# A SwiGLU feed-forward in two phases on Trainium2: gate and up of all columns first, then the down products as seven block products with seven open sums in PSUM

## What is computed

```python
def swiglu(h, w_in, w_out):
    gate, up = jnp.split(h @ w_in, 2, axis=-1)
    return (jax.nn.silu(gate) * up) @ w_out

cond = jax.nn.silu(c)
for l in range(DEPTH):
    mod = cond @ ada_w[l] + ada_b[l]
    sh0, sc0, gt0, sh1, sc1, gt1, sh2, sc2, gt2 = jnp.split(mod, 9, axis=-1)
    h = modulate(rms_norm(x, norm_g[l, 0]), sh0, sc0)
    x = x + (0.5 * (1 + gt0))[:, None, :] * swiglu(h, ffn_w_in[l, 0], ffn_w_out[l, 0])
    ...
    h = modulate(rms_norm(x, norm_g[l, 2]), sh2, sc2)
    x = x + (0.5 * (1 + gt2))[:, None, :] * swiglu(h, ffn_w_in[l, 1], ffn_w_out[l, 1])
```

## Time and profile before

| | us |
|---|---|
| three runs of the kernel before | 1482.46, 1481.02, 1480.61 |
| median | 1481.02 |
| span of the profiled execution (its time apart from the span is not listed; the three runs lie 0.6 to 2.5 above the span) | 1480.0 |
| TensorE matmul busy | 1457.4 (98%) |
| weight loads busy | 1327.5 (90%) |
| VectorE busy | 996.7 (67%) |
| ScalarE busy | 269.8 (18%) |
| SP's queue moved | 211.12 MB in 287168 packets |

### The profile page before, as it was taken

One profiled execution on the slowest core, in us unless ns is written; L12 is line 12 of the kernel. 1 busy time (PEld: TensorE's weight loads), 2 busy tenths in 40 slices (PEclk: granted clock), 3 DMA queues, 4 the chain that ended last, 5 costly groups with the idle time before them and its releaser, 6 DMA issues.

```text
span 1480.0 us, 27488 instructions
## 1 busy us (share of the span) xinstructions
PE 1457.4 (98%) x11800; PEld 1327.5 (90%) x11800; DVE 996.7 (67%) x1973; ACT 269.8 (18%) x542; POOL 74.7 (5%) x141
## 2 busy tenths in 40 slices
PE   6999999999999999999999999999999999999998
PEld 3999999888988989999989999988898889899997
DVE  6489987788534657888866767777963445555455
ACT  2100002442223030000030000035222311100001
POOL 7001110000000000000100000000000000000000
PEclk9999999999999999999999999999999999999999
DMA  9899998343422567898856878644342248356550
GB/s 335 259 292 298 306 304 230 111 128 100 115 59 87 177 194 236 274 301 270 282 180 213 276 242 273 200 132 142 114 115 59 60 143 274 117 184 192 174 170 30
DMA packets 306233, 282.93 MB, mean 191 GB/s; under 512 B 15368, under 2 KB 269696, under 8 KB 306112
## 3 DMA queue, kind: packets, MB, share of 16 engines
q1 hardware_dynamic: 287168, 211.12, 47.6%
q0 software_dynamic: 17952, 69.21, 13.7%
q10 hardware_dynamic: 992, 0.85, 0.2%
HBM read 280.10 MB, written 1.05 MB: 190 GB/s over the span
## 4 chain that ended last, share of the span: by engine, by line
PE 96%; DMA 1%; DVE 1%; ACT 1%; SPq 1%; issue 0%; ACTq 0%; DVEq 0%
PE ps L1600 95%; DMA arena<-in_ada_w_dram 1%; PE ps L1604 1%; SPq L485 1%; DVE arena L1458 0%; ACT rs L618 0%; ACT hT L618 0%; DVE x L1002 0%; DVE hT L970 0%; DVE hT L1585 0%; DVE arena L1453 0%; ACT xn L618 0%; ACTq L237 0%; SPq L483 0%; SPq L482 0%
## 5 line engine op out<-in xcount | busy, mean ns | idle before, releaser
L1600 PE MATMUL ps<-hT,ring 128*128 128x128 f32 (+2 forms) x2528 | 427.5, 322 | 3.8 <-ACT hT L618 3.8
L1600 PEld LDWEIGHTS ps<-hT,ring 128*128 128x128 f32 (+1 forms) x2528 | 371.7, 191 | 49.5 <-issue 10.7
L1600 PE MATMUL ps<-arena,ring 128*128 128x256 f32 (+2 forms) x1712 | 372.7, 370 | 0.0
L1600 PEld LDWEIGHTS ps<-arena,ring 128*128 128x128 f32 x1712 | 309.2, 190 | 36.7
L1600 PE MATMUL ps<-y_both,arena 128*128 128x128 f32 x1920 | 228.5, 275 | 0.0
L1600 PEld LDWEIGHTS ps<-y_both,arena 128*128 128x128 f32 x1920 | 221.1, 192 | 0.2
L939 DVE SCALAR_TENSOR_TENSOR ada_acc<-ada_stage,cond,ada_acc 128x512 f32<-128x512 f32 x231 | 173.6, 751 | 9.0 <-DMA ada_stage<-in_ada_w_dram 1.1
L1028 DVE TENSOR_TENSOR arena<-arena,ps 128x256 f32<-128x256 f32 x80 | 33.5, 419 | 171.6 <-ACT arena L661 171.6
L1600 PE MATMUL ps<-y_both,ring 128*128 128x128 f32 (+1 forms) x896 | 140.5, 305 | 0.0
L1600 PEld LDWEIGHTS ps<-y_both,ring 128*128 128x128 f32 x896 | 126.2, 191 | 6.4
L661 ACT ACTIVATE arena<-ps 128x128 f32<-128x128 f32 x80 | 22.2, 278 | 577.7 <-PE ps L1600 577.7
(11 more groups left out here) (280 smaller groups left out, 1172.4 us busy)
## 6 DMA issues: line engine op xcount, KB each, us to landing
ring<-in_ffn_w_in_dram SPq DMA_DIRECT2D x176, 512.0 KB, 5.4
ada_stage<-in_ada_w_dram POOLq DMA_DIRECT2D x66, 1024.0 KB, 6.9
ring<-in_ffn_w_out_dram SPq DMA_DIRECT2D x88, 512.0 KB, 6.7
ring<-in_mix_w_in_dram SPq DMA_DIRECT2D x46, 512.0 KB, 5.1
ring<-in_mix_w_in_dram SPq DMA_DIRECT2D x12, 1024.0 KB, 5.3
ring<-in_mix_w_in_dram SPq DMA_DIRECT2D x6, 1536.0 KB, 6.4
ring<-in_mix_w_out_dram SPq DMA_DIRECT2D x8, 1024.0 KB, 5.2
arena<-in_ada_w_dram SPq DMA_DIRECT2D x6, 1024.0 KB, 17.2
```

The lines of the kernel that those rows point to most:

```text
L1600: return nc.tensor.matmul(out_, lhsT, rhs, start=start, stop=stop, **kw)
```

## The change

Each half is cut in two phases, and chunks go by **pairs** (256 hidden columns).

- Phase 1 makes gate and up of all 22 chunks. The first two are done plainly, the other ten pairs by seven block products of eight matmuls each (the same matmuls as before, two chunks at a time, in four PSUM banks; two sets of four banks take turns). The weight sums are 128 x 1024 now and made in two parts (`weight_sums(..., late)`), and the results stay in SBUF, in the new `hidT` of 22 tiles.
- Phase 2 makes the down products by the same block scheme: a pair of chunks is the inner dimension, two halves of the 1024 outputs and two halves of the tokens are the others. So a pair takes 7 x 4 = 28 matmuls of 128 tokens, where it took 16 of 256. Each of the seven products accumulates over the eleven pairs in its own PSUM bank and is combined only once, at the end (`residual`). VectorE makes four sums of weight blocks a pair (`down_sums`, 128 x 512) and the token sums of `hidT` (`t_sums_of`, in four batches).
- The last three pairs' products are reordered so that the seven sums close one after another.
- `ring` becomes 12 cells of 1024 elements: an up pair takes four, a down pair two, the mixer's blocks three. There are eight landing semaphores instead of four.
- The units of `ada_w` become 256 x 1024 elements (still 1 MB), two sweeps of 128 x 1024 each; they stand at eleven steps of phase 1 and seven of phase 2 (`ADA_PLACES`).
- Small tiles move to other memory (`parts`, `sil`, `scaled`, `final_diag`).

```diff
-SLOTS = 4
+PAIRS_FF = NC // 2
+STEPS = PAIRS_FF + 1
+RING_CELLS = 12
...
+T_BATCHES = ((0, 3), (3, 7), (7, 10), (10, 11))
...
+ADA_PLACES = [("up", s, 4.4) for s in range(1, STEPS)] + [("down", p, 2.4) for p in range(7)]
...
             def ffn(l, half):
-                for c in range(NC):
-                    chunk(l, half, c)
+                for p in range(PAIRS_FF):
+                    use, col = up_use(half, p), 2 * P * p
+                    room(l, use)
+                    win = ffn_w_in[l:l + 1, half, :, :].rearrange("a (k p) (g n) -> p (a k) g n", p=P, g=2)
+                    for g in range(2):
+                        sp.dma_start(up_weights(l, half, p)[:, :, g, :], win[:, :, g, col:col + 2 * P])\
+                          .then_inc(full_of(l, use), 16)
+                for p in range(PAIRS_FF):
+                    use, row = down_use(half, p), 2 * P * p
+                    room(l, use)
+                    sp.dma_start(view(slot(l, use, 2048), 2, D),
+                                 ffn_w_out[l:l + 1, half, row:row + 2 * P, :].rearrange("a (c p) n -> p (a c) n", p=P))\
+                      .then_inc(full_of(l, use), 16)
...
+            def ffn_up(l, half, before):
+                for s in range(STEPS):
...
+                        link(l, V.tensor_tensor(parts[:, 0:2, :], parts[:, 7:8, :].broadcast_to([P, 2, 2 * P]),
                                                 both[:, 1:5:3, :], ALU.add))
...
+                        free(V.tensor_tensor(parts[:, 5, :], parts[:, 2, :], both[:, 5, :], ALU.add),
+                             f"combined {half}" if p == PAIRS_FF - 1 else None)
+                        weight_sums(l, half, p + 2, 0)
...
+                    weight_sums(l, half, p + 2, 1)
+                    if p == PAIRS_FF - 2:
+                        for q in range(2):
+                            down_sums(l, half, q)
+                    if p == 7:
+                        t_sums_of(l, half, 0)
+                    ada_at(l, half, "up", s)
+
+            def ffn_down(l, half):
+                t_sums_of(l, half, 1)
+                for p in range(PAIRS_FF - 2):
+                    dv.wait_ge(*PE.at(l, f"sums read {half} {p}"))
+                    down_sums(l, half, p + 2)
+                    if p == 3:
+                        t_sums_of(l, half, 2)
+                        t_sums_of(l, half, 3)
+                    ada_at(l, half, "down", p)
...
+            def residual(l, half, name):
+                c11, c12, c21, c22 = (quarters[:, k, :, t, :] for k in range(2) for t in range(2))
...
+                link(l, V.tensor_tensor(c12, c11, quad(1), ALU.add))
...
+                link(l, V.tensor_tensor(c21, c12, quad(2), ALU.add))
...
+                free(V.tensor_tensor(c12, c12, quad(3), ALU.add))
+                link(l, V.tensor_tensor(c22, c21, quad(3), ALU.add))
...
+                def added(k, part, t, label=None):
+                    new = x[:, k, t]
+                    free(V.scalar_tensor_tensor(new, part, gate_c[:, k:k + 1], new, ALU.mult, ALU.add), label)
...
+                for k in range(4, KT):
+                    added(k, quad(6)[:, k - 4, :], slice(0, P), f"x {name} {k // 2}" if k % 2 else None)
...
-                def down(c):
-                    w = view(ring[:, slot_of(l, use0 + c), 2048:3072], 8, P)
-                    pe.wait_ge(hid_ready, n0 + c + 1)
-                    for k in range(KT):
-                        last = mm(duo(k // 2)[:, k % 2, :], w[:, k, :], hid[:, c % 2, :],
-                                  start=(c == 0 and k % 2 == 0), stop=(c == NC - 1), skip_group_check=True)
...
+                def down_product(number, p):
+                    w = down_weights(l, half, p)
...
+                    bank, a, b, sums = {1: (0, a11, b11, 0), 6: (1, s2, t2, 3), 7: (2, s3, t3, 2), 5: (3, s1, t1, 1),
+                                        2: (4, a12, b21, 0), 3: (5, s4, b22, 4), 4: (6, a22, t4, 0)}[number]
...
+                    if sums:
+                        pe.wait_ge(w_summed, 4 * SUMS_BEFORE[l, half, "down", p] + sums)
+                    for i in range(4):
+                        last = mm(quad(bank)[:, i, :], a[:, i, :], b, start=(p == i == 0),
+                                  stop=(p == PAIRS_FF - 1), skip_group_check=True)
...
+                for p in range(1, PAIRS_FF):
+                    (up_pair_of_seven if seven(l, half, p) else up_pair)(p)
+                    owed[0] = True
+                end = PAIRS_FF - 1
+                pe.wait_ge(hid_ready, n0 + STEPS - 1)
+                for p in range(end - 2):
+                    for number in (1, 7, 6, 5):
+                        down_product(number, p)
+                    if p == 0:
+                        pe.wait_ge(*DV.at(l, f"combined {half}"))
+                    for number in (3, 2, 4):
+                        down_product(number, p)
+                for number in (1, 7, 6, 5, 3):
+                    down_product(number, end - 2)
+                last_sums()
+                for number, p in ((1, end - 1), (1, end), (6, end - 1), (7, end - 1), (5, end - 1), (6, end), (7, end),
+                                  (5, end), (2, end - 2), (2, end - 1), (2, end), (3, end - 1), (3, end),
+                                  (4, end - 2), (4, end - 1), (4, end)):
+                    down_product(number, p)
```

More of the change, by code:

```diff
@@ new lines, in ffn, with used, up @@
+                owed = [False]
+                def used(ins, k):
+                    if k == 0 and owed[0]:
+                        ins.then_inc(slot_free, 1)
+                        owed[0] = False
+                def up(s):
+                    w = up_weights(l, half, 0)
+                    if s == 0:
+                        pe.wait_ge(*landed(l, up_use(half, 0)))
+                        if before[1] != "start":
+                            ahead(*before, lambda k: w[:, k, 0, 0:P], lambda k: w[:, k, 1, 0:P]).then_inc(gu_ready, 1)
+                            return
@@ L1668, in up, with up_pair @@
                                       stop=(k == KT - 1))
                     last.then_inc(gu_ready, 1)
-                def up_of_seven(c, w):
+                def up_pair(p):
+                    w = up_weights(l, half, p)
+                    pe.wait_ge(*landed(l, up_use(half, p)))
+                    pe.wait_ge(hid_ready, n0 + p)
+                    for c in range(2):
+                        for g in range(2):
+                            for k in range(KT):
+                                last = mm(duo(up_bank(p) + c)[:, g, :], w[:, k, g, c * P:c * P + P], hT[:, k, :],
+                                          start=(k == 0), stop=(k == KT - 1))
+                                used(last, k)
+                    last.then_inc(gu_ready, 1)
```

607 lines of the change are left out of this document (346 added, 261 removed).

## The result

The changed kernel takes 1468.56 us (median of four runs, 1467.85 to 1470.33), beside 1481.74 for the kernel before in the same session: a ratio of 0.9911, with a 95% interval from 0.9899 to 0.9923. It is faster by 13.2 us. The forecast was 1465.4, 3.2 us lower, in a range from 1453 to 1478.

A forecast was written before the change was run, and what follows sets the result against it. TensorE, busy 98% of the span, was taken as the bound. 29.5 - 8.3 - 0.7 - 3.2 - 1.7 = 15.6 us took the span from 1480.0 to 1464.4, so the median to 1465.4 us, range 1453 to 1478.

The forecast's parts named there:

- The product: 29.5: TensorE's down products: 6.92 us a pair falls to 6.25, over 44 pairs 29.5 us less.
- First half: 8.3 + 0.7 of waits: TensorE waits 8.3 us for VectorE's combination at down pair 0's fifth product, and some 0.7 later in phase 2.
- the sweep at 1.30: VectorE's price for a 128x1024 sweep of `ada_w`, taken as 1.31 us start to start, bounds 1.23 and 1.55.
- the early idling of 4.0: VectorE idles 4.0 us early in the first half, while still ahead of TensorE.
- Second half: 1.0 + 2.2: TensorE waits 1.0 us for the combination, then 2.2 at down sums of pair 2 and the next pair; 3.2 together.
- no wait for landings: VectorE would not wait for loads to land; loads were taken at 0 us, bounds 0 and 1.6.
- The clock: 1.7, "and nothing for the small waits": After the first half's gap TensorE's clock falls, costing 1.7 us; small waits cost nothing. Bounds 0 and three times that.
- the distance of the median from the span: The median of the runs lies 1.0 us above the profiled span.
- The end of a half at nothing: Extra multiply-adds after the last down matmul are covered by next-stage matmuls: cost nothing, bounds 0 and 1 us each.
- The rival "loads become the bound": In phase 1 `weight_sums` wait for up-weight loads; 0.8 us a pair cancels the gain, 1.5 gives 1495; chance 0.08.

The follow-up runs named there:

- b2: Changed kernel with both phases kept but down products plain: 16 full products of 256 tokens a pair, no down or token sums; 1481.60 us.
- a1: Changed kernel with first-half `ada_w` units of steps 9 and 10 (one each) moved into the down phase; 1465.05 us.
- b3: Changed kernel with up pair 1 of the first half made by 32 full products instead of seven block products; 1470.17 us.
- a2: Changed kernel with up pair 10 of the first half made by 32 full products instead of seven block products; 1464.36 us.
- a3: Changed kernel with layer 0's `ada_w` units (all but the first two) loading 64 of 1,024 columns, sweeps and waits kept; 1465.95 us.
- a4: Changed kernel with 32 extra, repeated products in the first half's down pair 0, filling TensorE's wait; 1467.67 us.
- d1: a2 with one step 11 `ada_w` unit moved to the down phase in both layer 0 halves, and one of step 9 in the first; 1457.34 us.
- c2: a2 with the first half's `ada_w` units (all but the first two) loading 64 of their 1,024 columns; 1460.69 us.
- b4: Changed kernel with two first-half `ada_w` units moved from steps 8 and 9 to steps 1 and 2; 1467.56 us.
- b1: Changed kernel with products 1, 7, 6, 5 of down pairs 0 and 1 made before the wait for up pair 10's combination, all halves; 1467.48 us.
- c1: a2 with up pair 10 of the second half also made by full products; 1467.42 us.

## Why the prediction was right, and where not

- **The product: 29.5.** 28 matmuls take 6.25 us, at the pitch taken from the earlier trace rows. Run b2 is 13.0 us above the changed kernel; with what the latter loses in its first two halves (7.57 + 1.5, and 0.98 + 1.99 + 1.7, together 13.7) that is 26.7. In the third half, where nothing waits, TensorE went from 217.25 us (761.67 to 978.92) to 210.15 (762.15 to 972.30), 7.1 less where 7.4 was forecast. So the term was right within a tenth.
- **First half: 8.3 + 0.7 of waits.** Measured 7.57 at the place named, and no second wait. The sum of VectorE's work was right, with the sweep at 1.30 and the early idling of 4.0 (1.7 and 2.3). That it is a sum over the phase, and not the work next to the boundary, is now shown by a1 (moved: comes back), b3 (taken out too early: nothing) and a2.
- **Second half: 1.0 + 2.2.** Measured 0.98 + 1.99, and that the sizes agree is luck. The prediction had VectorE's own queue in both. Without late landings (a3) its own queue makes 0.4, 0.2 and 1.58 us at the sums of pair 3, some 2.2 in all. The landings add 2.85, which the prediction had at nothing ("no wait for landings"). That is the step that failed: it is nearly the whole size of the 3.2 us by which the forecast was too low.
- **The clock: 1.7, "and nothing for the small waits".** In the first half the rows give 1.5, a4 about 1.0. In the second the clock fell too, behind a wait of 2 us, which the prediction did not expect; but the half was not longer for it (table under a4), so leaving it out did no harm.
- **Where the 3.2 us lie.** The span fell by 13.2, not 15.6. The first half was to change by +3.3 and went from 225.60 to 227.61, +2.0, since its waits were smaller. The second was to change by -4.2 and changed by -1.8: the 2.4 between are 2.85 of landings, less 1.0 for the smaller waits of its own queue, 0.3 for the product, and 0.3 without a place. The third and fourth were to give 14.7 and gave 13.9 with the end. A start 0.3 later and the mixers, 0.2, make up the sum. The last 0.8 is the distance of the median from the span, 1.8 instead of 1.0. So a first half that was forecast too long hid part of the miss in the others.
- **The end of a half at nothing.** From the first matmul on the squares (`ones`) to the next stage's first with `hT` it is 3.20 us in both kernels, 975.72 to 978.92 before and 969.10 to 972.30 after. Right.
- **The rival "loads become the bound".** It did not decide the sign, and its place (`weight_sums` waiting for up weights) showed no wait. Its kind was right: the loads are a bound, but through the adaLN units and around the phase boundary.

## What to carry to other kernels

When TensorE meets a queue on another engine at one point, add up that engine's work from where it last idled. Here work taken out before that point was worth nothing (b3), and most of the work moved behind it came back as waits (a1). Then look what stands in the queue between the meeting point and the next result that is needed: a step that waits for a transfer there holds up everything behind it. Here the units that are loaded around the boundary were such a step, and one unit moved behind the next two results gave 4.5 us (d1). And before a stretch at half rate is counted as a loss, ask which engine sets the pace behind it: in the second half it was VectorE, and the stretch cost nothing.

## What the runs showed of the hardware

- **The length of a wait does not tell whether the clock falls.** Half rate (granted clock down to 0.50) followed waits of 1.99 us in the changed kernel, 2.34 (a1), 2.43 (a2) and 2.76 (c2), when TensorE was already busy. It did not follow waits of 2.11 and 2.21 (a1), 2.24 (b3) and 3.02 (b4), where the clock stayed at 1.00.
- **Half rate can cost nothing.** Five of the nine second halves in the table have a stretch with 1.7 us or so of lost clock, four have none, and the lengths less the landings agree within 0.12 us.
- **A shorter wait can lose more clock.** Half rate held from about 185.2 to 192.0 us in the changed kernel and from 185.6 to 192.4 in b1, though TensorE was back 2.1 us sooner in b1. The loss is the work that falls into the stretch: 1.5 us with a wait of 7.57, 2.7 with one of 3.58.
- **The clock at the start varies.** All fourteen profiled executions have the clock below 1.00 between 30 and 32 us. In eight TensorE ran at half rate again between 36 and 42 us, as in the earlier trace rows; in four the first stretch reached to 34 us and there was no second, and a2 and b1 have neither, with the changed kernel's program up to there. The Trainium skill, page "TensorE: Matmul & The Clock Gate", Part 1, says the same of a kernel's start, that the number of slow matmuls differs from run to run; the traces agree, and it is worth up to 1.8 us here (up pair 1's product with the token sums begins between 54.55 and 56.39 us). So a profiled span can mislead by that much: a2's is 1461.0, while its other runs were 1.1 to 2.0 us above it, though what made these longer is not shown.
- **Landing times at full load.** The transfers of the units, all of 1 MB, took between 5.2 and 12.6 us in c1. Up to 800 us, those of 10 us and more had the 16 engines at 0.85 to 1.03 of their time in the 8 us from their issue. But one of 5.6 us (issued at 63.63) had them at 0.99, so full engines alone do not make a landing late, and some of the slow ones (10.2 us, issued at 116.23 and 128.91) fell in the middle of a phase, where nothing waited long for them.
